# A fused two-block transformer kernel: one 512-column matmul for two of 256 in the up and down stages

## The chip, the cores and the metric

The kernel runs on one core of one Trainium2 chip. The metric is the device time of one execution in microseconds (us). The kernel before took 1595.41 us, the median of three runs. A core has a matrix engine (PE, with PEld for its weight loads), VectorE (DVE), ScalarE (ACT), GpSimd (POOL) and a queue (SP) that issues the weight transfers. TensorE's clock has two levels here, 1.2 and 2.4 GHz; the profile gives it as the granted share, 0.50 or 1.00.

## What is computed

256 tokens of width 1024 go through four layers of attention and gated feed-forward, and then through a second block of one layer. The part that the change touches is the feed-forward:

```python
def conv_gated_ffn(h, w_up, conv_w, conv_b, w_down):
    u = h @ w_up
    C = u.shape[-1]
    u = lax.conv_general_dilated(u, conv_w[:, None, :].astype(u.dtype), window_strides=(1,),
                                 padding=[(CONV_W - 1, 0)], dimension_numbers=('NWC', 'WIO', 'NWC'),
                                 feature_group_count=C) + conv_b
    gate, val = jnp.split(u, 2, axis=-1)
    return (jax.nn.silu(gate) * val) @ w_down
```

D_FF is 2752 (21.5 tiles of 128) in these four layers. In the second block (`conv_ffn`) D_FF is 2816, only the gate passes the three-tap convolution, the activation is a GELU, and the value half multiplies it unconvolved.

## The kernel before

Activations lie transposed: 128 features on the partitions, 256 tokens (S) in a row. All matrix products are made in float32r with both operands split into a high and a low part, `w_hi`, `w_lo` and `h_hi`, `h_lo` (in the down stage `act_hi`, `act_lo`), and three matmuls of 256 columns stand for one product: high by high, high weights by low activations, low weights by high activations. This is `product` (lines 1480, 1481 and 1482); such a group of three is called a triple below, with 128 by 128 weights of its own for each of its matmuls. The first two chunks of an up stage go through `pair` and `first_outputs` (lines 1515 and 1524), which take the tiles of h as they come.

Weights come from memory in 225 chunks, through a ring of three slots (`w_raw`, `w_hi`, `w_lo`). SP loads a chunk when the low part of the chunk three before it is made; ACT copies it to `w_hi` (line 321) when PE has used the chunk three before; DVE subtracts to get `w_lo` (line 804), and PE's `chunk_ready` waits for that. Stages follow one another: mixer projections and attention, `wo` (output projection), `up` (22 chunks), `down` (8 chunks). A chunk of `up` is 16 triples: 8 for a gate tile into a bank of `pj`, 8 for a value tile into a bank of `val_bank`. In the first four layers chunk 21, the last, holds half tiles and is 8 triples. A chunk of `down` is 22 triples into one bank.

Beside PE each chunk of `up` has a step on each engine, with no scheduler: the order is as the code is written, with semaphores. `used` counts finished chunks. ACT's step j writes tap 2 and the bias of both tiles from PSUM to `cgate` and `cval` (line 733), makes the high part of chunk j+3 (`next_split`), and applies Silu to the gate (line 737). DVE's step adds the other two taps of both tiles from PSUM (line 1242, four instructions), makes the low part of chunk j+3, and multiplies gate and value (line 1259). POOL's step (`split_act`, lines 1451 and 1454) makes `act_hi` and `act_lo` of the product. Chunk 0 of `up` was computed from h without its norm factor, so its step first multiplies by `rstd` (line 1234). Steps 1 to 18 lie in a hardware loop of six turns of three steps, on ACT and on DVE; steps 0 and 19 to 21 stand outside it.

PE starts `down` with the first 19 triples of two chunks, and then waits for `act_free`, that is for POOL's last step, before their last three. DVE adds each finished chunk from PSUM to `x` (line 1279); ACT's squares and the next stage's raw h follow it.

## Time and profile before

| | |
|---|---|
| three runs, us | 1595.56, 1595.41, 1593.86 |
| span of the profiled execution | 1593.4 us |
| PE busy | 1536.5 us, 96% |
| DVE busy | 1037.6 us, 65% |
| ACT busy | 861.8 us, 54% |
| POOL busy | 315.3 us, 20% |
| chain that ended last | PE 83%, DVE 9%, ACT 4% |
| DMA | mean 166 GB/s |

The span is the profiled execution's own time; it lies 2.0 us below the median of the runs. Matmuls are pipelined, and the duration of one (283 ns) includes the way through the array, so their rate is read from the distance between starts. The same holds to a lesser degree for DVE and ACT, where neighbours overlap by some 0.08 us.

### The profile page before, as it was taken

The page shows a single profiled execution, that of the slowest core. Times are in us where ns is not written, and L with a number is a line of the kernel's source. Part 1 is how long each engine was busy: PE and PEld are TensorE (multiplying, and loading weights), DVE is VectorE, ACT ScalarE, POOL GpSimd, SP SyncE. Part 2 cuts the span into 40 slices and gives each one's busy share as a digit, 9 for nine tenths or more (in the row PEclk, how much of TensorE's full clock was granted, in tenths as well). Part 3 has the DMA queues.
Part 4 walks back from the last instruction along what each step waited for, and adds up shares of the span by engine and source line. Part 5 has one row for each costly group of instructions (what it writes and reads, how often), then busy time and mean ns, then how long its engine had stood idle before and what let it go on. Part 6 is the DMA issues. An engine that isn't in the chain of part 4 may idle for free.

```text
span 1593.4 us, 32385 instructions
## 1 busy us (share of the span) xinstructions
PE 1536.5 (96%) x12270; PEld 1483.0 (93%) x12270; DVE 1037.6 (65%) x1639; ACT 861.8 (54%) x1347; POOL 315.3 (20%) x474
## 2 busy tenths in 40 slices
PE   6999999999999999989999999999999897899998
PEld 5989999999999999978999999899999897899997
DVE  5668876553378765567877466688765655866555
ACT  4766555455565554455656446665554455544533
POOL 2103211212222112112212220022110360211100
PEclk9999999999999999999999999999999899899999
DMA  7543556443336564442656445435564253355550
GB/s 256 169 159 117 205 183 241 152 159 118 119 113 207 183 243 152 132 159 80 211 184 219 178 148 167 160 116 205 182 243 152 96 196 106 129 188 194 189 205 27
DMA packets 36669, 264.70 MB, mean 166 GB/s; under 512 B 4767, under 2 KB 4826, under 8 KB 7792
## 3 DMA queue, kind: packets, MB, share of 16 engines
q1 hardware_dynamic: 33552, 255.59, 45.8%
q0 software_dynamic: 3040, 8.05, 2.0%
q8 instruction: 52, 0.85, 0.2%
q14 instruction: 25, 0.20, 0.0%
HBM read 262.50 MB, written 1.12 MB: 165 GB/s over the span
## 4 chain that ended last, share of the span: by engine, by line
PE 83%; DVE 9%; ACT 4%; issue 2%; DMA 1%; SPq 0%; POOL 0%; ACTq 0%; DVEq 0%
PE bank L1480 26%; PE bank L1481 24%; PE bank L1482 24%; PE bank L1515 2%; DVE w_lo L804 2%; DVE tmp L853 2%; ACT tmp L395 1%; PE bank L1524 1%; DVE acc L841 1%; PE bank L1623 1%; ACT w_hi L321 1%; DVE tmp L885 1%; PE bank L1591 1%; DVE w_lo L813 1%; DMA w_raw<-w_std 1%
## 5 line engine op out<-in xcount | busy, mean ns | idle before, releaser
L804 DVE TENSOR_TENSOR w_lo<-w_raw,w_hi 128x2048 fp32r<-128x2048 f32 (+2 forms) x220 | 543.3, 2472 | 221.4 <-ACT w_hi L321 221.2
L1480 PE MATMUL bank<-h_hi,w_hi 128*128 128x256 f32 x2032 | 579.0, 285 | 1.3 <-DVE w_lo L804 1.3
L1481 PE MATMUL bank<-h_lo,w_hi 128*128 128x256 f32 x2032 | 574.9, 283 | 0.0
L1482 PE MATMUL bank<-h_hi,w_lo 128*128 128x256 f32 x2032 | 574.9, 283 | 0.0
L321 ACT CAST w_hi<-w_raw 128x2048 fp32r<-128x2048 f32 (+2 forms) x220 | 445.2, 2024 | 5.7 <-DMA w_raw<-w_std 2.9
L1480 PEld LDWEIGHTS bank<-h_hi,w_hi 128*128 128x128 f32 x2032 | 389.6, 192 | 6.7 <-issue 4.1
L1481 PEld LDWEIGHTS bank<-h_lo,w_hi 128*128 128x128 f32 x2032 | 389.7, 192 | 0.1
L1482 PEld LDWEIGHTS bank<-h_hi,w_lo 128*128 128x128 f32 x2032 | 389.6, 192 | 0.0
L1480 PE MATMUL bank<-act_hi,w_hi 128*128 128x256 f32 x1220 | 355.9, 292 | 5.7 <-DVE act_lo L957 4.2
L1481 PE MATMUL bank<-act_lo,w_hi 128*128 128x256 f32 x1220 | 345.7, 283 | 0.0
L1482 PE MATMUL bank<-act_hi,w_lo 128*128 128x256 f32 x1220 | 345.5, 283 | 0.0
L1480 PEld LDWEIGHTS bank<-act_hi,w_hi 128*128 128x128 f32 x1220 | 233.9, 192 | 20.1 <-DVE act_lo L957 6.0
L1481 PEld LDWEIGHTS bank<-act_lo,w_hi 128*128 128x128 f32 x1220 | 234.4, 192 | 0.1
L1482 PEld LDWEIGHTS bank<-act_hi,w_lo 128*128 128x128 f32 x1220 | 234.5, 192 | 0.0
L733 ACT ACTIVATE tmp<-bank,par 128x256 f32<-128x256 f32 x181 | 93.6, 562 | 227.9 <-PE bank L1482 227.3
L1242 DVE SCALAR_TENSOR_TENSOR tmp<-bank,par,tmp 128x255 f32<-128x255 f32 (+1 forms) x362 | 155.6, 478 | 85.0 <-ACT tmp L733 82.3
L1451 POOL CAST act_hi<-tmp 128x256 f32 x110 | 43.6, 397 | 482.6 <-DVE tmp L1259 372.3
L351 ACT ACTIVATE sq<-x 128x256 f32<-128x256 f32 (+1 forms) x67 | 31.9, 479 | 166.7 <-DVE x L1279 154.7
L1353 POOL TENSOR_SCALAR proj<-x,par 128x256 f32<-128x256 f32 x35 | 44.4, 1270 | 327.7 <-ACT h_hi L379 327.7
L1515 PE MATMUL bank<-h_hi,w_hi 128*128 128x256 f32 x320 | 94.0, 312 | 12.8 <-ACT h_hi L375 7.3
L1515 PE MATMUL bank<-h_hi,w_lo 128*128 128x256 f32 x320 | 90.3, 301 | 0.0
L1454 POOL TENSOR_TENSOR act_lo<-tmp,act_hi 128x256 f32 x110 | 81.4, 740 | 17.6 <-POOL act_hi L1451 17.2
(162 smaller groups left out, 1754.1 us busy)
## 6 DMA issues: line engine op xcount, KB each, us to landing
w_raw<-w_std SPq DMA_DIRECT2D x181, 1024.0 KB, 4.9
w_raw<-w_down SPq DMA_DIRECT2D x40, 1408.0 KB, 6.0
w_raw<-w_gate SPq DMA_DIRECT2D x4, 1280.0 KB, 5.4
act_hi<-vec_dram POOLq DMA_DIRECT2D x28, 128.0 KB, 3.1
act_lo<-vec_dram POOLq DMA_DIRECT2D x28, 128.0 KB, 3.6
x<-xT SPq DMA_DIRECT2D x2, 512.0 KB, 4.7
out<-x SPq DMA_DIRECT2D x4, 256.0 KB, 2.4
par<-params SPq DMA_DIRECT2D x1, 499.0 KB, 9.3
```

The costliest lines, as they stand in the source:

```text
L321: act.copy(w_hi[:, slot, 0:width], w_raw[:, slot, 0:width]).then_inc(hi_ready, 1)
L351: act.activation(sq[:, n, to:end], source, ACT.Square).then_inc(sq_ready, 1)
L733: act.activation(to[:, slot, :], source, ACT.Identity, bias=col(3), scale=col(2)).then_inc(conv_init, 1)
L804: dve.tensor_tensor(w_lo[:, slot, 0:width], w_raw[:, slot, 0:width], w_hi[:, slot, 0:width].bitcast(F32), ALU.subtract).then_inc(lo_ready, 1)
L1242: return dve.scalar_tensor_tensor(to[:, slot, lag:S], source(v)[:, 0:S - lag], par[:, bass.ds(at + (4 * v + 2 - lag), 1)], to[:, slot, lag:S],
L1353: pool.tensor_scalar(proj[:, k % 4, :], x[:, k, :], gain_of(app, k), None, ALU.mult)\
L1451: pool.tensor_copy(act_hi[:, bass.ds(j, 1), :].squeeze(1) if not isinstance(j, int) else act_hi[rows, j, :], cval[rows, slot, :]).then_inc ...
L1454: pool.tensor_tensor(act_lo[rows, j, :], cval[rows, slot, :], act_hi[rows, j, :].bitcast(F32), ALU.subtract).then_inc(act_free, 1)
L1480: pe.matmul(dst, wh, xh, start=first, stop=False, skip_group_check=shared)
L1481: pe.matmul(dst, wh, xl, start=False, stop=False, skip_group_check=shared)
L1482: done = pe.matmul(dst, wl, xh, start=False, stop=last, skip_group_check=shared)
L1515: pe.matmul(dst, a, b, start=k == 0 and w is wh and (n == 0 or not shared), stop=False, skip_group_check=shared)
```

## The change

- `h_hi` and `h_lo`, and `act_hi` and `act_lo`, become halves of one tensor each (`h_both`, `act_both`), so that high and low lie side by side as 512 columns. `wide_product` makes a triple from two matmuls: low weights by the high 256 columns, then high weights by all 512. The second leaves high by high in the left half of a bank and high by low in the right half. It is used in all `up` stages and in the `down` stages of the first four layers: 4 x 344 + 352 = 1728 triples of `up` and 4 x 176 = 704 of `down`, 2432 in all.
- `pj` and `val_bank` are interleaved, so that a chunk's two banks are neighbours. In `up`, ACT first copies both right halves to `up_sum` (512 columns, signal `low_taken`), DVE adds both left halves (512 columns, signal `bank_free`), and bias, taps and the value read SBUF. In `down`, DVE adds the two halves to `x` one after the other.
- DVE no longer multiplies gate and value; POOL does, ahead of its two split instructions.
- DVE's step makes the low part of the chunk two ahead, not three, and makes it ahead of the taps. Step 0 makes none, and one more stands behind step 21.
- ACT's Silu of tile j-1 is now in step j, between the copy and the bias instructions.

The new helper on PE:

```diff
+            def wide_product(bank, weights, moving, start, stop):
...
+                for k, ((wh, wl), (xh, pair)) in enumerate(zip(weights, moving)):
+                    pe.matmul(bank[:, 0:S], wl, xh, start=start and k == 0, stop=False, skip_group_check=True)
+                    done = pe.matmul(bank[:, :], wh, pair, start=False, stop=stop and k == len(weights) - 1,
+                                     skip_group_check=True)
+                return done
```

ACT's step in `up`:

```diff
+                            act.copy(up_sum[:, slot, :, :], halves(slot, S)).then_inc(low_taken, 1)
+                        if before is not None:
+                            activate(*before)
+                        if isinstance(j, int) and j == 0:
+                            act.wait_ge(first_scaled, ffn + 1)
+                        else:
+                            act.wait_ge(bank_free, c + (RING + 1))
...
+                            act.activation((cgate, cval)[v][:, slot, :], up_sum[:, slot, v, :], ACT.Identity,
...
                         split()
```

DVE's step in `up`:

```diff
+                        dve.wait_ge(low_taken, n_ + 1)
...
+                            dve.tensor_tensor(up_sum[:, slot, :, :], halves(slot, 0), up_sum[:, slot, :, :], ALU.add)\
+                               .then_inc(bank_free, 1)
                         if first:
...
+                            dve.tensor_tensor(up_sum[:, slot, :, :], up_sum[:, slot, :, :],
+                                              rstd[:, :].unsqueeze(1).broadcast_to([P, 2, S]), ALU.mult)\
+                               .then_inc(first_scaled, 1)
+                        split()
...
+                    def split_two_ahead(j, i=None):
+                        n_ = c0 + j + 2
+                        split_lo(n_ if i is None else i * RING + n_, n_ % RING, SIZES[n_])
```

DVE in `down`, and POOL's step in `up`:

```diff
                             dve.tensor_tensor(x[:, k, :], pj[slot_of(c0, k)][:, 0:S], x[:, k, :], ALU.add)\
+                               .then_inc(x_main, 1)
+                            dve.wait_ge(x_main, layer * DT + k + 1)
+                            dve.tensor_tensor(x[:, k, :], pj[slot_of(c0, k)][:, S:2 * S], x[:, k, :], ALU.add)\
                                .then_inc(bank_free, 1)
...
+                        pool.wait_ge(gated, n_ + 1)
...
+                        pool.tensor_tensor(cval[rows, slot, :], cgate[rows, slot, :], value, ALU.mult)\
+                            .then_inc(prod_done, 1)
```

One step of DVE in the loop of `up`, before (`bank` is PSUM, `tmp` holds `cgate` and `cval`):

```order
L1242 SCALAR_TENSOR_TENSOR tmp<-bank,par,tmp 128x255
L1248 REGISTER_ALU
L1242 ISA [waits conv_init]
L1242 SCALAR_TENSOR_TENSOR tmp<-bank,par,tmp 128x255
L1250 ISA
L1242 ISA [waits conv_part]
L1242 SCALAR_TENSOR_TENSOR tmp<-bank,par,tmp 128x254
L1253 REGISTER_ALU
L1242 ISA [waits conv_part]
L1242 SCALAR_TENSOR_TENSOR tmp<-bank,par,tmp 128x254
L803 REGISTER_ALU
L804 TENSOR_TENSOR w_lo<-w_raw,w_hi 128x2048 [waits hi_ready]
```

The same step of DVE with the change (`held` holds `up_sum`):

```order
L1237 TENSOR_TENSOR held<-psum,held 128x512 [waits low_taken]
L817 REGISTER_ALU
L818 TENSOR_TENSOR w_lo<-w_raw,w_hi 128x2048 [waits hi_ready]
L1260 ISA
L1248 ISA [waits conv_init]
L1248 SCALAR_TENSOR_TENSOR tmp<-held,par,tmp 128x255
L1260 REGISTER_ALU
L1248 ISA [waits conv_init]
L1248 SCALAR_TENSOR_TENSOR tmp<-held,par,tmp 128x255
L1263 ISA
L1248 ISA [waits conv_part]
L1248 SCALAR_TENSOR_TENSOR tmp<-held,par,tmp 128x254
```

The sum and the weights' low part stand ahead of the taps, the taps read SBUF alone, and the multiplication (L1259, the row behind the first piece) is gone.

ACT at the end of step 0 and in the first step of the loop of `up`, before:

```order
L733 ACTIVATE tmp<-u_sb,par 128x256 [waits first_scaled]
L321 CAST w_hi<-w_raw 128x2048 [waits arrived1,used]
L737 ACT_TABLE_LOAD
L737 ACTIVATE tmp<-tmp 128x256 [waits conv_part]
L744 UNCONDITIONAL_BRANCH
L744 ISA
L724 REGISTER_ALU [waits used]
L733 ISA [waits act_free]
L733 ISA
L733 ACTIVATE tmp<-bank,par 128x256
```

The same place with the change:

```order
L747 ACTIVATE tmp<-held,par 128x256
L331 CAST w_hi<-w_raw 128x2048 [waits arrived1,used]
L757 UNCONDITIONAL_BRANCH
L757 ISA
L734 REGISTER_ALU [waits used]
L738 ACT_TABLE_LOAD
L738 COPY held<-psum 128x512 [waits act_free]
L726 ISA
L727 ACT_TABLE_LOAD
L727 ACTIVATE tmp<-tmp 128x256 [waits conv_part]
```

The one table load that stood ahead of the loop has become two inside it, which every turn runs again.

The end of `up` on DVE, before; the three rows of `w_lo` with 2816 columns are the first three chunks of `down`:

```order
L1242 SCALAR_TENSOR_TENSOR tmp<-bank,par,tmp 128x255 [waits conv_init] x2
L1242 SCALAR_TENSOR_TENSOR tmp<-bank,par,tmp 128x254 [waits conv_part] x2
L804 TENSOR_TENSOR w_lo<-w_raw,w_hi 128x2816 [waits hi_ready]
L1259 TENSOR_TENSOR tmp<-tmp 128x256 [waits bank_free,gated]
L1242 SCALAR_TENSOR_TENSOR tmp<-bank,par,tmp 128x255 [waits conv_init] x2
L1242 SCALAR_TENSOR_TENSOR tmp<-bank,par,tmp 128x254 [waits conv_part] x2
L804 TENSOR_TENSOR w_lo<-w_raw,w_hi 128x2816 [waits hi_ready]
```

The same with the change:

```order
L1237 TENSOR_TENSOR held<-psum,held 128x512 [waits low_taken]
L818 TENSOR_TENSOR w_lo<-w_raw,w_hi 128x2048 [waits hi_ready]
L1248 SCALAR_TENSOR_TENSOR tmp<-held,par,tmp 128x255 [waits conv_init] x2
L1248 SCALAR_TENSOR_TENSOR tmp<-held,par,tmp 128x254 [waits conv_part] x2
L1237 TENSOR_TENSOR held<-psum,held 128x512 [waits low_taken]
L818 TENSOR_TENSOR w_lo<-w_raw,w_hi 128x2816 [waits hi_ready]
L1248 SCALAR_TENSOR_TENSOR tmp<-held,par,tmp 128x255 [waits conv_init] x2
L1248 SCALAR_TENSOR_TENSOR tmp<-held,par,tmp 128x254 [waits conv_part] x2
L1234 TENSOR_TENSOR held<-psum,held 128x256 [waits low_taken]
```

The first pieces of both begin with step 19. The first chunk of `down` was split in step 19 and is now split in step 20.

## Rows read from the trace of the kernel before

**Rows 1.** The page: span, and busy time of each engine.

```profile
span 1593.4 us, 32385 instructions
PE 1536.5 (96%) x12270; PEld 1483.0 (93%) x12270; DVE 1037.6 (65%) x1639; ACT 861.8 (54%) x1347; POOL 315.3 (20%) x474
```

**Rows 2.** Groups by line and shape: count, then busy us, mean ns, idle before.

```profile
L443 ACT COPY vtok<-bank 128x512 f32<-128x512 f32 x15 | 8.5, 570 | 4.0 <-PE bank L1482 4.0
...
L1175 DVE TENSOR_TENSOR x<-bank,x 128x512 f32<-128x512 f32 x12 | 7.9, 685 | 7.6 <-PE bank L1482 7.6
...
L737 ACT ACT_TABLE_LOAD x5 | 6.4, 1283 | 0.1
```

**Rows 3.** Timeline of PE in an up stage: start, duration; 48 matmuls between starts.

```profile
250.08 0.28 PE L1480 MATMUL bank<-h_hi,w_hi 128*128 128x256 f32 x1
...
255.84 0.28 PE L1480 MATMUL bank<-h_hi,w_hi 128*128 128x256 f32 x1
```

**Rows 4.** Timeline of PEld: weight loads of plain float32 matmuls, and the next load.

```profile
1258.45 0.84 PEld L1591 LDWEIGHTS bank<-sq,cst 128*128 128x128 f32 x4
1259.31 0.19 PEld L1515 LDWEIGHTS bank<-h_hi,w_hi 128*128 128x128 f32 x1
```

**Rows 5.** Timeline of PE: two float32r matmuls while the granted clock is 0.50.

```profile
745.58 0.41 PE L1515 MATMUL bank<-h_hi,w_lo 128*128 128x256 f32 x1
745.80 0.41 PE L1515 MATMUL bank<-h_hi,w_hi 128*128 128x256 f32 x1
```

**Rows 6.** Timeline of DVE: one whole step of the loop of up.

```profile
161.29 1.65 DVE L1242 SCALAR_TENSOR_TENSOR tmp<-bank,par,tmp 128x255 f32<-128x255 f32 x4
162.85 2.28 DVE L804 TENSOR_TENSOR w_lo<-w_raw,w_hi 128x2048 fp32r<-128x2048 f32 x1
165.05 0.42 DVE L1259 TENSOR_TENSOR tmp<-tmp 128x256 f32<-128x256 f32 x1
```

**Rows 7.** Timeline of POOL as up begins in layer 0.

```profile
148.02 0.75 POOL L1341 TENSOR_TENSOR h_lo<-tmp,h_hi 128x256 fp32r<-128x256 f32 x1 [0.80 <-ACT h_hi L375]
```

**Rows 8.** Timeline of DVE as up begins in layer 0 (brackets: idle before).

```profile
148.10 2.82 DVE L804 TENSOR_TENSOR w_lo<-w_raw,w_hi 128x2048 fp32r<-128x2048 f32 x1
150.85 0.74 DVE L1234 TENSOR_TENSOR u_sb<-bank,rstd 128x256 f32<-128x256 f32 x2
...
154.31 2.29 DVE L804 TENSOR_TENSOR w_lo<-w_raw,w_hi 128x2048 fp32r<-128x2048 f32 x1 [0.53 <-ACT w_hi L321]
```

**Rows 9.** Timeline of ACT as up begins in layer 0, and in step 20.

```profile
151.38 1.10 ACT L733 ACTIVATE tmp<-u_sb,par 128x256 f32<-128x256 f32 x2 [3.43 <-DVE u_sb L1234]
152.38 1.90 ACT L321 CAST w_hi<-w_raw 128x2048 fp32r<-128x2048 f32 x1
...
260.72 1.02 ACT L733 ACTIVATE tmp<-bank,par 128x256 f32<-128x256 f32 x2 [1.99 <-PE bank L1482]
```

**Rows 10.** Timeline of DVE, step 19: the first chunk of down.

```profile
258.45 3.09 DVE L804 TENSOR_TENSOR w_lo<-w_raw,w_hi 128x2816 fp32r<-128x2816 f32 x1 [1.18 <-ACT w_hi L321]
```

**Rows 11.** Timeline of POOL: the end of its step in the loop of up.

```profile
161.54 0.40 POOL L1451 CAST act_hi<-tmp 128x256 f32 x1 [3.11 <-DVE tmp L1259]
162.10 0.74 POOL L1454 TENSOR_TENSOR act_lo<-tmp,act_hi 128x256 f32 x1 [0.16 <-POOL act_hi L1451]
```

**Rows 12.** Stretches: length, busy us of each engine (count), PEclk, DMA share, GB/s.

```profile
157.00:265.00 108.00, 108.00 (x902) 108.00 (x902) 84.79 (x119) 63.37 (x80) 22.77 (x40) 1.00 0.58 202
...
741.30:744.30 3.00, 1.35 (x5) 0.59 (x4) 2.42 (x5) 1.65 (x5) 2.43 (x3) 1.00 0.38 161
744.40:747.50 3.10, 3.10 (x12) 2.92 (x13) 2.88 (x4) 2.18 (x4) 0.00 (x0) 0.50 0.00 0
747.70:751.00 3.30, 3.30 (x29) 3.30 (x28) 3.30 (x7) 2.26 (x6) 1.83 (x2) 0.98 0.71 228
```

**Rows 13.** Timeline of DVE in down, layer 0: two additions to x in a row.

```profile
285.30 0.42 DVE L1279 TENSOR_TENSOR x<-bank,x 128x256 f32<-128x256 f32 x1
...
292.05 0.42 DVE L1279 TENSOR_TENSOR x<-bank,x 128x256 f32<-128x256 f32 x1
```

212 lines of the change are left out of this document (103 added, 109 removed).

## Prediction

> **What bounds the kernel now.** I read the page first: PE is busy 96% of the span of 1593.4 us [rows 1]. Then the stretches: in 108 us of the up stage of layer 0 PE has no idle time at all, while DVE is busy 85 us, ACT 63 and POOL 23 [rows 12]. So in `up` a saved PE nanosecond is gained until DVE's own work for a chunk is longer than PE's. The timelines give both. PE: 48 matmuls, one chunk, lie between 250.08 and 255.84, so 5.76 us a chunk, 0.120 a matmul, 0.360 a triple [rows 3]. DVE: the taps take 1.56 us from start to start, the low part of the weights 2.20 [rows 6]. The sums below are of one profiled execution; its span is 2.0 us below the median of the runs, and I add that back at the end.
>
> **A triple on PE.** The columns stay 768, and a weight load goes. At the granted clock of 0.50 two matmuls start 0.22 us apart, close to 256 columns at 1.2 GHz (0.213) [rows 5]. At 2.4 GHz 256 columns would be 0.107, but the row has 0.120: here something other than columns adds 13 ns [rows 3]. Whether it adds them to 512 columns too, no float32r row tells. The nearest are the four plain float32 matmuls, which start 0.86/4 = 0.215 us apart at full clock, with a weight load each: as long as 512 columns take (0.213), with only 2 ns above them [rows 4]. So I take 0.216 for the wide one and 0.120 for the narrow: 0.336 a triple, 24 ns less. The ends are 0.213 (0.333) and, if the extra is in proportion to the columns, 0.240 (0.360, no gain); between them lies 0.227 (0.347), a fixed 13 ns. Over 2432 triples the 24 ns would be 58 us.
>
> The Trainium skill (TensorE: Matmul & The Clock Gate, Back-to-back issue gap) gives N/2.4 + 2.5 ns for matmuls in a row. By it 256 columns take 109 ns and 512 take 216, and this change would bring only 2.5 ns a triple, 6 us in all. For 256 columns the trace disagrees (120), so its rule against the change falls for the narrow ones; for 512 no run here shows it yet.
>
> **DVE's step in up.** It loses the multiplication and gains a sum of 512 columns: 0.685 us by its group, 0.60 without the overlap of neighbours [rows 2]. So 0.60 + 2.20 + 1.56 = 4.36 us, against PE's 16 x 0.336 = 5.38. But the taps now read SBUF twice, not PSUM, and POOL has a third instruction. A POOL subtraction starts at 148.02 and takes 0.75; DVE's instruction with two SBUF inputs starts at 148.10 and takes 2.82, not 2.28 [rows 7, 8]. So POOL held it up for 0.54 us, until 0.62 after its own start. In `up` before, POOL's two lie beside taps from PSUM, which keep their pace (1.65 for four) [rows 6, 11]. Now two such POOL instructions and a cast (0.40, perhaps 0.3 of it) can delay DVE by up to 1.5 a step; the least is 0. The product mostly begins while DVE is in the sum, which reads PSUM, so I take 1.0: 5.36, a tie with PE. With the table loads below I take **5.45 us a chunk** for chunks 2 to 20; the ends are 5.38 and 5.8.
>
> **ACT.** The order of instructions shows two table loads in the loop where one stood ahead of it: 1.283 us each [rows 2], 2.6 us in three steps. ACT had 63 busy of 108 us, and its step grows by a 512-column copy (0.57 [rows 2]) and 0.85 of loads: from 3.4 to 4.8 of 5.4 us. It hides, except where ACT's copy releases DVE: one sum in three comes 1.3 us later.
>
> **The start of up.** After the low part of chunk 2 is ready at 150.85, PE works on it for 5.76, until 156.6; that of chunk 3 is ready at 154.31 + 2.2 = 156.5, just in time [rows 8]. Now it stands in step 1, behind this chain from 150.85: DVE sum and scaling of 512 columns 1.3; ACT's two bias instructions 1.0 and high part 1.9 [rows 9]; table load 1.3; copy 0.55; DVE's sum 0.65; low part 2.2. That is 8.9, against 5.4 for PE's chunk: **a wait of 3.5 us** in each of layers 0 to 3, and 3.0 in layer 4, which has one bias instruction. Chunks 0 and 1 gain nothing: the low part of chunk 2 is late behind them already.
>
> **The end of up.** Chunk 20 ends at 260.7 [rows 9], and the first chunk of `down` is ready at 258.45 + 3.0 = 261.5, 2.1 us before PE has done the half chunk 21 [rows 10]. Now its low part is made in step 20: copy 0.6, sum 0.65, 3.0, so 4.3 after chunk 20, where PE is done after 2.7. The wait is 1.6 if DVE is in time, and 3.1 to 3.7 if it lags. I take **2.5**, in layers 0 to 3 only: layer 4 has a whole chunk 21. POOL's longer last step is hidden by PE's 2 x 19 triples, 12.8 us.
>
> **Down.** 176 x 0.024 = 4.2 us less in each of four layers. DVE's and ACT's round there is 292.05 - 285.30 = 6.75, and 7.1 with the second addition [rows 13]; PE's chunk of 22 triples falls to 7.4 and covers it. Behind the last chunk PE has the next stage's raw tiles, except after layer 3: there the addition adds 0.4.
>
> **The clock.** After 3 us in which PE was busy 1.35, the granted clock was 0.50 for 3.1 us: 12 matmuls instead of 26 [rows 12]. One such fall costs 1.6 us. A wait of 3.5 should bring it in all five layers; in four of them DVE catches up meanwhile, so I count 1.2 there. For the wait at the end I count half of it, 0.8.
>
> **The sum.** A layer of the first four: 19 x (5.45 - 5.76) = -5.9; chunk 21 -0.2; down -4.2; start +3.5; end +2.5; clock +2.0: together -2.3, times four -9.2. Layer 4: 20 x 0.384 = -7.7, start +3.0, clock +1.6: -3.1. End of layer 3 +0.4. Together -11.9: a span of 1581.5, and 1583.5 beside the median. The case's own range is 1574 to 1592.
>
> **Rivals.**
> - **POOL makes DVE the bound (slower).** The delay is 1.4 a step: 5.75 us a chunk. Then 19 chunks give -0.2, the end wait is 3.7, and the clock at the start costs nothing more: -0.2 - 0.2 - 4.2 + 3.5 + 3.7 + 0.8 = +3.4 a layer, +13.6, and with layer 4 and the 0.4 about +11: 1606. It decides from 5.6 us a chunk on, since each 0.1 is 7.6 us. For it: the 0.54 us of delay [rows 7, 8]. Against: only if all three POOL instructions meet DVE's. Chance 0.18. The Trainium skill (SBUF — State Buffer, Who interferes with whom) has the rule: a DVE instruction with two SBUF inputs and a GpSimd instruction that reads SBUF exclude each other for the whole instruction; the trace agrees, with 0.62 of 0.75 us.
> - **The wide matmul costs 0.240.** Nothing is gained on PE; the waits stay (3.1, 1.5, clock 1.9 a layer; 4.2 in layer 4): +31, 1626. Against it: the 0.215 us [rows 4]. Chance 0.07.
> - **It costs 0.227.** Chunks at 5.55: -4.0 - 0.1 - 2.3 + 3.3 + 2.1 + 1.7 = +0.7 a layer, layer 4 about 0, and 0.4: +3, 1599, at the edge of no change. Chance 0.14.
> - **No contention and no clock fall to speak of.** 5.38 a chunk, end wait 1.6: -7.3 - 0.2 - 4.2 + 3.5 + 1.6 = -6.6 a layer, -26; layer 4 -4.7: -31, 1565; with the falls at the start 1573. Chance 0.24.
>
> The forecast has 0.37. Faster by over 0.2% (under 1592.2; about what a measurement can tell from no change): 0.55, the forecast but for its edge and the last rival. Within 0.2%: 0.13. Slower: 0.32, from the first two and half of the third. The range is 1565 to 1609; it leaves out the second rival and the ends of the first and last.
>
> **What would show it.** Wide matmuls followed by the next start after 0.216 us; used chunks 5.4 to 5.5 apart in `up`; PE waiting some 3.5 us for `w_lo` ahead of chunk 3 in five layers, and 2 to 3 us ahead of `down` in four; a granted clock of 0.50 behind them; 60 table loads of 1.28 us in the loops; low parts of 2.8 us on DVE where POOL is at work. The prediction is wrong if DVE never idles in `up`, or if the wide matmuls start 0.24 apart.

## The result, and the profile after

The changed kernel took **1609.5 us**, the median of four runs (1608.2 to 1610.5), beside 1595.3 for the kernel before (four runs, 1593.9 to 1595.6). The ratio is 1.0091, with a 95% interval of 1.0077 to 1.0105: slower by 0.9%, 14 us. The prediction had 1583.5 and "faster". The page after, its span and busy times, against [rows 1]:

```profile
span 1608.7 us, 27907 instructions
PE 1523.7 (95%) x9838; PEld 1348.0 (84%) x9838; DVE 1166.1 (72%) x1666; ACT 1006.1 (63%) x1512; POOL 584.1 (36%) x584
```

PE has 2432 matmuls fewer and is busy for 13 us less in a span that is 15 us longer. So PE waits more, and what it does takes longer than was forecast.

**PE's price.** Its timeline in `up` of layer 1, in two stretches of the same stage (start, duration; of each triple its narrow matmul, the first of its two):

```profile
500.04 0.28 PE L1501 MATMUL psum<-h_both,w_lo 128*128 128x256 f32 x1
...
500.73 0.28 PE L1501 MATMUL psum<-h_both,w_lo 128*128 128x256 f32 x1
...
560.13 0.28 PE L1501 MATMUL psum<-h_both,w_lo 128*128 128x256 f32 x1
...
561.19 0.28 PE L1501 MATMUL psum<-h_both,w_lo 128*128 128x256 f32 x1
```

Around 500 two triples take 0.69 us, and over a chunk 5.55: 0.347 a triple. From the start of a narrow matmul to that of the wide one are 0.117 us, from there to the next narrow one 0.230. Around 560 three triples take 1.06 us: 0.353, or 5.66 a chunk; there the wide matmul has 0.236. Before, a triple took 0.360 [rows 3]. The prediction took 0.336. The two distances, 5.55 and 5.66 us a chunk, are called the short and the long cadence below.

**The waits.** PE's waits for the low parts of the weights, over the whole span (us in all, times, longest of them). The four that the view puts down to "issue" are those ahead of `down`:

```profile
PE psum L1501 <- DVE w_lo L818: 16.3, 8, 3.3
...
PE psum L1501 <- issue: 9.4, 4, 2.4
```

Windows of PE in layer 0: ahead of chunk 3 and behind it; then in layer 1: ahead of `down` and behind its start (busy us and count of PE, PEld, DVE, ACT, POOL; then the granted clock):

```profile
156.00:159.50 3.50, 0.76 (x5) 0.40 (x3) 2.42 (x2) 3.46 (x6) 0.55 (x1) 1.00 0.00 0
159.50:163.00 3.50, 2.97 (x10) 2.59 (x11) 3.50 (x6) 2.95 (x4) 2.23 (x4) 0.51 0.54 152
588.90:591.60 2.70, 0.36 (x3) 0.06 (x2) 2.70 (x2) 2.70 (x2) 2.70 (x1) 1.00 0.55 234
593.00:596.40 3.40, 3.40 (x13) 2.81 (x12) 3.40 (x4) 2.63 (x3) 2.41 (x1) 0.50 0.88 358
```

The first wait is 3.2 to 3.3 us in layers 0 to 3 and 2.6 in layer 4, the second 2.4 in layers 0 to 3. Behind the first of layers 0, 1 and 2 and behind all four of the second there are 3.4 us at a granted clock of 0.50 (1.2 GHz), in which PE does half its work: 1.4 to 1.8 us more each. None of these nine waits is in the kernel before.

The chain of the first wait, on DVE and ACT in layer 0 (brackets: idle before, and its releaser):

```profile
150.81 0.68 DVE L1237 TENSOR_TENSOR held<-psum,held 128x512 f32<-128x512 f32 x1
...
157.08 0.69 DVE L1237 TENSOR_TENSOR held<-psum,held 128x512 f32<-128x512 f32 x1 [2.42 <-ACT held L738]
157.69 2.28 DVE L818 TENSOR_TENSOR w_lo<-w_raw,w_hi 128x2048 fp32r<-128x2048 f32 x1
```

```profile
155.17 1.28 ACT L738 ACT_TABLE_LOAD   x1
156.46 0.59 ACT L738 COPY held<-psum 128x512 f32<-128x512 f32 x1
```

It is the chain of the prediction: 157.69 + 2.2 = 159.9 is 9.1 us behind 150.81 (8.9 forecast), while PE has work for 5.55.

**DVE in `up`**, one step of the steady state, and POOL beside it:

```profile
538.30 2.60 DVE L818 TENSOR_TENSOR w_lo<-w_raw,w_hi 128x2048 fp32r<-128x2048 f32 x1
540.82 2.34 DVE L1248 SCALAR_TENSOR_TENSOR tmp<-held,par,tmp 128x255 f32<-128x255 f32 x4
543.08 0.68 DVE L1237 TENSOR_TENSOR held<-psum,held 128x512 f32<-128x512 f32 x1
543.68 2.60 DVE L818 TENSOR_TENSOR w_lo<-w_raw,w_hi 128x2048 fp32r<-128x2048 f32 x1
```

```profile
543.39 0.74 POOL L1459 TENSOR_TENSOR tmp<-tmp 128x256 f32<-128x256 f32 x1 [1.30 <-ACT tmp L727]
544.30 2.24 POOL L1462 CAST act_both<-tmp 128x256 f32 x1 [0.17 <-POOL tmp L1459]
546.72 0.74 POOL L1465 TENSOR_TENSOR act_both<-tmp,act_both 128x256 f32 x1 [0.18 <-POOL act_both L1462]
```

From one low part to the next are 5.38 us: the low part takes 2.60 and the four taps 2.34, where they took 2.28 and 1.65 [rows 6]. POOL's product (543.39) delays the low part by 0.3, its subtraction (546.72) the taps by 0.7. The cast delays nobody, but is itself held up while DVE makes the low part: 2.24 us instead of 0.40 [rows 11]. The Trainium skill (SBUF — State Buffer, Who interferes with whom) says that a DVE instruction with two SBUF inputs contends with a GpSimd instruction that reads SBUF, and that the lock is exclusive. The trace agrees for POOL's product and subtraction, in both directions; the cast is shut out (2.24 us), but shuts nobody out.

That step has no table load. A turn of the loop, three steps, has two. DVE's sums behind the load, in two turns in a row of layer 1, and PE at the chunk whose low part ends at 538.30 + 2.60 = 540.90:

```profile
515.44 0.69 DVE L1237 TENSOR_TENSOR held<-psum,held 128x512 f32<-128x512 f32 x1 [0.30 <-ACT held L738]
...
532.13 0.69 DVE L1237 TENSOR_TENSOR held<-psum,held 128x512 f32<-128x512 f32 x1 [0.30 <-ACT held L738]
```

```profile
541.03 0.31 PE L1501 MATMUL psum<-h_both,w_lo 128*128 128x256 f32 x1
...
541.40 0.28 PE L1501 MATMUL psum<-h_both,w_lo 128*128 128x256 f32 x1
```

A turn takes 16.69 us, 5.56 a chunk, where 5.45 was forecast, and in it (504 to 541) neither ACT nor DVE waits for PE. Three short chunks of PE are 16.64. So while PE keeps the short cadence, DVE with ACT's table loads is as much the bound of `up` as PE: the first triple of chunks 7, 10 and 13 takes 0.37 to 0.40 us for 0.347. In the long cadence (16.97) DVE has 0.3 us in hand.

**Stage by stage.** PE's first matmul of `up`, of `down`, and of the next stage, in layer 1, before and after:

```profile
458.78 0.78 PE L1515 MATMUL bank<-h_hi,w_hi 128*128 128x256 f32 x1
...
582.41 0.28 PE L1480 MATMUL bank<-act_hi,w_hi 128*128 128x256 f32 x1
...
648.66 0.38 PE L1515 MATMUL bank<-h_hi,w_hi 128*128 128x256 f32 x1
```

```profile
463.25 0.74 PE L1543 MATMUL psum<-h_both,w_lo 128*128 128x256 f32 x1
...
591.61 0.36 PE L1501 MATMUL psum<-act_both,w_lo 128*128 128x256 f32 x1 [2.35 <-issue]
...
657.74 0.38 PE L1546 MATMUL psum<-h_both,w_hi 128*128 128x256 f32 x1
```

`up` went from 123.6 to 128.4 us, `down` from 66.3 to 66.1. Layer 0 has +5.1 and -0.3. In all, layers 0 to 3 bring 4.8, 4.3, 4.3 and 4.0 us, and the rest of the program -2.1 (before, layer 4 begins with 17.1 us at the lower clock; after, with 10.2 and 3.4): 15.3 us of span.

### The profile page after: what moved, and what is told of

It is laid out like the page before. It is cut to its first block, busy times and chain, and to the rows that moved or that the text cites. A ratio compares the mean times of both kernels' runs of the same rounds, so it can differ in the third digit from the quotient of the medians.

```text
span 1608.7 us, 27907 instructions
## 1 busy us (share of the span) xinstructions
PE 1523.7 (95%) x9838; PEld 1348.0 (84%) x9838; DVE 1166.1 (72%) x1666; ACT 1006.1 (63%) x1512; POOL 584.1 (36%) x584
## 4 chain that ended last, share of the span: by engine, by line
PE 75%; DVE 14%; ACT 6%; issue 4%; DMA 1%; POOL 0%; ACTq 0%; SPq 0%; DVEq 0%
PE psum L1502 32%; PE psum L1501 17%; PE psum L1491 7%; PE psum L1492 7%; PE psum L1493 7%; DVE w_lo L818 4%; DVE tmp L867 3%; ACT w_hi L331 1%; ACT tmp L405 1%; DVE acc L855 1%; PE psum L1655 1%; DVE tmp L899 1%; DVE h_both L863 1%; DVE w_lo L827 1%; DMA w_raw<-w_std 1%
## 5 line engine op out<-in xcount | busy, mean ns | idle before, releaser
L1502 PE MATMUL psum<-h_both,w_hi 128*128 128x512 f32 x1568 | 556.0, 399 | 0.0
L1501 PE MATMUL psum<-h_both,w_lo 128*128 128x256 f32 x1568 | 443.1, 283 | 16.3 <-DVE w_lo L818 16.3
L1502 PEld LDWEIGHTS psum<-h_both,w_hi 128*128 128x128 f32 x1568 | 296.5, 189 | 71.7
L1501 PEld LDWEIGHTS psum<-h_both,w_lo 128*128 128x128 f32 x1568 | 298.2, 190 | 20.3 <-DVE w_lo L818 19.8
L1502 PE MATMUL psum<-act_both,w_hi 128*128 128x512 f32 (+1 forms) x704 | 254.0, 400 | 0.0
L1248 DVE SCALAR_TENSOR_TENSOR tmp<-held,par,tmp 128x255 f32<-128x255 f32 (+1 forms) x388 | 242.2, 673 | 6.6 <-ACT tmp L747 3.4
L1501 PE MATMUL psum<-act_both,w_lo 128*128 128x256 f32 (+1 forms) x704 | 206.5, 293 | 9.4 <-issue 9.4
L1462 POOL CAST act_both<-tmp 128x256 f32 x110 | 178.2, 1620 | 18.9 <-POOL tmp L1459 18.5
L1491 PE MATMUL psum<-act_both,w_hi 128*128 128x256 f32 x516 | 150.4, 292 | 5.8 <-DVE act_both L971 4.1
L1492 PE MATMUL psum<-act_both,w_hi 128*128 128x256 f32 x516 | 146.4, 284 | 0.0
L1491 PE MATMUL psum<-h_both,w_hi 128*128 128x256 f32 x464 | 135.1, 291 | 0.9 <-DVE w_lo L818 0.9
L1492 PE MATMUL psum<-h_both,w_hi 128*128 128x256 f32 x464 | 131.2, 283 | 0.0
L1493 PE MATMUL psum<-h_both,w_lo 128*128 128x256 f32 x464 | 131.1, 283 | 0.0
```

Of the source, the lines that this page charges most:

```text
L1248: return dve.scalar_tensor_tensor(to[:, slot, lag:S], up_sum[:, slot, v, 0:S - lag], par[:, bass.ds(at + (4 * v + 2 - lag), 1)], to[:, slo ...
L1462: pool.tensor_copy(act_hi[:, bass.ds(j, 1), :].squeeze(1) if not isinstance(j, int) else act_hi[rows, j, :], cval[rows, slot, :]).then_inc ...
L1491: pe.matmul(dst, wh, xh, start=first, stop=False, skip_group_check=shared)
L1492: pe.matmul(dst, wh, xl, start=False, stop=False, skip_group_check=shared)
L1493: done = pe.matmul(dst, wl, xh, start=False, stop=last, skip_group_check=shared)
L1501: pe.matmul(bank[:, 0:S], wl, xh, start=start and k == 0, stop=False, skip_group_check=True)
```

## The experiments

The theory, **edges**: PE is still the bound inside `up`; the wide matmul saves 7 to 13 ns a triple and not 24; and the loss is made at the two edges of each `up`, where the later low parts make PE wait and its clock falls. The rivals: **DVE**, slowed by POOL, has become the bound of `up`; or **ACT**, by its table loads, has. The times are medians of four executions (ten for e1 and e5, seven for e3 and e9, five for e8), and each ratio is to runs of the kernel before on the same chip. Waits, clock falls and cadences are those of the one profiled execution. The diffs are cut to what matters; comments in them are added.

| run | edit | us | ratio to before (95%) |
|---|---|---|---|
| changed kernel | | 1609.5 | 1.0091 (1.0077, 1.0105) |
| e1 | start of `up`: chunk 3 split in step 0 | 1593.2 | 0.9990 (0.9979, 1.0001) |
| e2 | end of `up`: low parts earlier | 1614.3 | 1.0135 (1.0109, 1.0161) |
| e3 | e1 and e2 | 1601.0 | 1.0045 (1.0027, 1.0063) |
| e4 | wide matmuls as two of 256 (not in chunks 0 and 1 of `up`) | 1625.6 | 1.0200 (1.0181, 1.0218) |
| e5 | no table loads in the loop | 1593.9 | 0.9996 (0.9985, 1.0006) |
| e6 | DVE multiplies | 1606.6 | 1.0064 (1.0039, 1.0089) |
| e7 | wide matmuls in `down` alone | 1588.0 | 0.9953 (0.9937, 0.9970) |
| e8 | e1 and e6 | 1589.5 | 0.9960 (0.9946, 0.9974) |
| e9 | e1 and e5 | 1590.0 | 0.9967 (0.9955, 0.9978) |
| e10 | e9, end of `up` on ACT and DVE | 1579.6 | 0.9904 (0.9887, 0.9920) |
| e11 | POOL's product twice | 1634.1 | 1.0243 (1.0226, 1.0260) |
| e12 | e10, one wait more | 1579.2 | 0.9893 (0.9868, 0.9917) |
| e13 | e12 again | 1576.3 | 0.9887 (0.9870, 0.9903) |
| e14 | e12, matmuls in the other order | 1583.1 | 0.9926 (0.9910, 0.9943) |

### e1: the start

```diff
 ACT, step 0
                         act.copy(up_sum ...)
+                        split()                       # high part of chunk 3
                         act.wait_ge(first_scaled, ffn + 1)
...
-                        split()
 DVE
-                    step(0, ..., lambda: None)
+                    step(0, ..., lambda: split_two_ahead(1))
+                    step(1, ..., lambda: None)
-                        for k in range(1, RING + 1):
+                        for k in range(2, RING + 2):
```

> The changed kernel (1609.5 us, span 1608.7) with one edit at the start of up: in step 0 ACT makes the high part of chunk 3 ahead of the bias instructions, DVE makes its low part behind the scaling, and step 1 makes none; all later steps are as they were. Theory, edges: PE is the bound inside up, and what the change lost are two waits a layer with a clock fall behind each. The start costs 3.2 us of waiting and 1.6 of half clock in layers 0 to 3, and about as much in layer 4: 5 x 4.8 = 24 us fewer at most, 20 if layer 4 keeps its fall: 1586 to 1590, the wait ahead of down stays at 2.4 us. Rival, DVE: DVE with its busy 98 of 102 us is the bound of up; the low part that is now earlier puts its step behind, PE waits 0.5 to 2 us inside up or more at the end: the gain is under half, 1598 or more. Rival, nothing: the chain is as long as before because DVE waits for ACT anyway: 1609.

1593.2 us, 16 less: short of the 20 to 24 expected, and more than either rival allows. The waits ahead of chunk 3 and the three clock falls behind them are gone. What is left (the same view as above):

```profile
PE psum L1505 <- issue: 9.3, 4, 2.4
...
PE psum L1505 <- DVE w_lo L821: 6.3, 8, 1.4
```

In each of the first four layers a wait of 1.2 to 1.4 us has come up ahead of chunk 4. The low part in step 0 makes DVE late for step 1, so the DVE rival holds for one chunk, not for the stage: the later chunks take 5.66. The sum, from the starts of chunks 2 to 5: 3.2 to 3.3 us in each of layers 0 to 2 (the wait shorter by 1.9, the rest the clock fall), 2.1 in layer 3, where no fall was to be saved, and 2.5 in layer 4. One fall ahead of `down` is gone too (1.6), and twelve chunks that had been short are long (less 1.3). That is 15, as the profiled spans have it (15.3).

### e2 and e3: the end, first try

```diff
                     for j in range(turns * RING + 1, n):
-                        step(j, ..., lambda: split_two_ahead(j))
-                    split_two_ahead(n)
+                        step(j, ..., lambda: split_two_ahead(j) if j < n - 2 else None)
+                        if j >= n - 3:
+                            split_two_ahead(j + 1)
```

> The changed kernel (1609.5 us) with one edit at the end of up: the low parts of the first three chunks of down are made behind the taps of steps 19, 20 and 21, as in the kernel before, and not ahead of the taps of steps 20 and 21 and behind step 21. Theory, edges: the wait of 2.4 us and the half clock behind it (1.6) go in four layers: 16 us fewer, 1593 to 1595. The wait at the start stays at 3.2. Rival, DVE: with the taps ahead of the low part the bias instruction (0.8 us of waiting) stands in the way and DVE is late with the second chunk of down or PE waits for the last products: half of the gain or less, 1601 or more.

1614.3 us: dearer by 0.44%, where a gain of 1% was expected. The wait ahead of `down` fell only from 2.4 to 1.4 us. The reason is in POOL and ACT in layer 1:

```profile
588.61 3.36 POOL L1460 TENSOR_TENSOR tmp<-tmp 128x256 f32<-128x256 f32 x1 [1.30 <-ACT tmp L727]
```

```profile
592.02 1.09 ACT L747 ACTIVATE tmp<-held,par 128x256 f32<-128x256 f32 x2 [3.58 <-DVE held L1237]
593.02 2.53 ACT L331 CAST w_hi<-w_raw 128x2816 fp32r<-128x2816 f32 x1
```

The low part, now ahead of the sum of step 20, holds back that sum by 3.0 us; ACT's bias waits 3.6 for it, and the high part of the second chunk stands behind the bias. POOL's product takes 3.4 us instead of 0.7, shut out by the low part. So two waits have taken the place of the one (low parts 17.8 us in 12 waits, up from 16.3 in 8; POOL):

```profile
PE psum L1502 <- POOL act_both L1466: 6.1, 4, 1.6
```

The edges failed. What the second theory said is what happened: the bias stands in the way, and PE waits for the last products; its 1601 or more holds too, by far. The clock shows what the edges had right. None of the eight waits (1.4 to 1.6 us) has a fall behind it, and `down` still takes 66.9 us for 66.1, since the waits inside it cost more than the fall. Layer 4, which the edit leaves as it was at its start, had a fall here (1.5 us) that it hadn't before. The end is no matter of one instruction's place.

> The changed kernel with both edits, at the start of up and at its end. Theory, edges: no wait for w_lo and no clock fall behind one is left in the first four layers; the two gains add: 24 + 16 = 40 us fewer, 1570 to 1574, which is below the kernel before (1595.3) by about 22: 2432 triples at 7 to 13 ns are 16 to 32. Rival, DVE: DVE has no slack left in up, so the low parts that are made earlier come back as waits inside up: 1585 or more, and PE's chunks in up are longer than 5.66 us in the mean.

1601.0 us, and not 1570 to 1574. The gain of the start is there and so is the loss of the end (0.55% above e1), so the edits add, but the second with its own sign. From chunk 5 on no chunk of `up` took more than 5.68 us (5.64 in the mean), so the rival that the earlier low parts come back as waits inside `up` fails.

### e4: the wide matmul's price

```diff
-                    done = pe.matmul(bank[:, :], wh, pair, ...)
+                    pe.matmul(bank[:, 0:S], wh, pair[:, 0:S], ...)
+                    done = pe.matmul(bank[:, S:2 * S], wh, pair[:, S:2 * S], ...)
```

> The changed kernel with every 512-column matmul of wide_product written as two of 256 with the same weights, into the same two halves of the bank; all else as it was. Theory, edges: a triple goes back to 0.360 us from 0.347 (0.353 in much of up), 2432 triples cost 16 to 32 us more, of which the waits give back some 3 because PE needs its weights later: 1622 to 1638. Rival, DVE: DVE's step is the bound of up, PE's longer chunks are hidden there and only the 704 triples of down show: 1614 to 1618. Rival, the wide matmul brings nothing: 1609.

1625.6 us, 16 more; triples take 0.360, in every stage. The sum: the edit reaches 2272 triples (chunks 0 and 1 go through another helper), and by 13 ns they are 30 us; 71 chunks of the changed kernel had the long cadence and lose only 0.1 (less 7.5); the waits are 0.2 to 0.3 shorter, since PE asks for its weights later (less 2), and three clock falls fewer lie behind those ahead of `down` (less 5): 15 to 16. So the wide matmul is worth some 22 us in these triples, and the theory's forecast holds. Two matmuls of 256 columns in a row with the same weights still take 0.120 each; each has a weight load of its own in the trace, so what a load kept for both would save isn't shown. Three narrow matmuls cost 40 ns above their columns at 2.4 GHz (0.360 for 0.320), a narrow and a wide one 27 (0.347). That is 13 ns a matmul at either width in the sum, neither the 2 ns that the prediction read from plain float32 [rows 4] nor an extra in proportion to the columns, which would leave 0.360. How the 27 are shared the starts don't say: they have 0.117 and 0.230, that is 10 and 17.

### e5: the table loads

```diff
+                    step(1, c0 + 1, ..., lambda: next_split(c0, 1), (0, slot_of(c0, 0)))
-                    turns = (n - 1 - RING) // RING
+                    turns = (n - 1 - RING) // RING - 1
-                        for k in range(1, RING + 1):
+                        for k in range(2, RING + 2):
```

> The changed kernel (1609.5 us) with ACT's step 1 taken out of the loop of up, whose turns become five (steps 2 to 16); the engine's state is then the same on entry and on each turn, and no table load stands in the loop: one of 1.28 us is left ahead of it, behind the copy of step 1. Theory, edges: inside up PE is the bound and the 60 loads cost nothing; only the copy of step 1 comes 1.3 us earlier, so the wait ahead of chunk 3 falls from 3.2 to 1.9 in five layers: 6.5 us fewer, 1603, a little less if some clock falls go too (1598). Rival, ACT: the loads (2.6 us in every three steps) hold back the sum, and with it DVE and PE; without them 15 us or more go: below 1594. Rival, nothing: 1609.

1593.9 us, 16 less, at least 4 more than the edges expected (6.5 to 11.5), and where the ACT rival had its mark. ACT and DVE behind chunk 2 of layer 0, then a window of layer 1 around the wait:

```profile
155.23 0.56 ACT L738 COPY held<-psum 128x512 f32<-128x512 f32 x1
155.81 1.28 ACT L727 ACT_TABLE_LOAD   x1
```

```profile
155.83 0.69 DVE L1238 TENSOR_TENSOR held<-psum,held 128x512 f32<-128x512 f32 x1 [1.00 <-ACT held L738]
```

```profile
474.00:477.50 3.50, 1.65 (x10) 1.20 (x9) 3.50 (x4) 3.49 (x5) 1.94 (x2) 1.00 0.01 2
```

The chain is shorter by the load ahead of the copy, as expected: the wait is 1.8 to 1.9 us, not 3.3, and in layer 4 1.3, not 2.6. What was not expected lies in the clock and the cadence. The clock stays at 1.00 behind the shorter wait, as in the window, in three of the four layers (in layer 2 it fell), and behind the waits ahead of `down` (2.1 us) it fell in two of four: three falls for seven. And four of the five `up` stages ran at 5.55 us a chunk, 51 chunks more than in the changed kernel. The sum: at the starts of the five stages 9 us, ahead of `down` 1 and behind it 3, by the short chunks 5 to 6; the profiled spans differ by 18.7 (1590.0; it is the second fastest execution of the ten, which spread over 8 us).

So the ACT rival is right in part. In the short cadence the loads held PE up themselves, but only by 0.03 to 0.05 us every third chunk (layer 1 of the changed kernel, above). The larger part goes by way of the cadence. In the changed kernel each change from the short cadence to the long one (chunk 13 of layer 1, chunk 7 of layers 2 and 3) stands at such a held-up triple, of 0.360 to 0.383 us. Over all runs, 4 of 31 stages with loads in the loop ran short from chunk 5 to their end (those of layers 0 to 3 of e11 left out), and 16 of 30 without. The runs without loads differ in other edits, too, so that the loads bring on the long cadence is likely and not shown.

### e6 and e8: POOL's product back on DVE

```diff
+                    def multiply(j, slot): ...       # on DVE, behind the low part of step j + 1
-                        pool.tensor_tensor(cval[rows, slot, :], cgate[rows, slot, :], value, ALU.mult)
```

> The changed kernel (1609.5 us) with the product of gate and value made by DVE again: the product of tile j-1 stands in DVE's step j behind the low part, and one more behind step 21; POOL makes only act_hi and act_lo. All else as it was. Theory, edges with POOL's lock as a cause of DVE's lateness: DVE's step gains 0.34 us and loses the 0.55 us or more by which the product holds up a low part or two taps; PE's pace in up stays at 5.55 to 5.66 us a chunk, the wait at the start stays 3.2, the wait at the end falls from 2.4 to about 2: 1604 to 1609. Rival, POOL is the bound of up: chunks of 5.65 become 5.55 and the end wait goes: 1594 or less. Rival, DVE's added instruction makes it the bound: 1615 or more.

1606.6 us. DVE's sum in two steps in a row:

```profile
174.28 0.69 DVE L1246 TENSOR_TENSOR held<-psum,held 128x512 f32<-128x512 f32 x1 [0.29 <-ACT held L738]
...
179.66 0.68 DVE L1246 TENSOR_TENSOR held<-psum,held 128x512 f32<-128x512 f32 x1
```

The step is 5.38 us, as without the edit: the product costs DVE 0.34 as its own work and 0.3 as a lock. The waits at the start stay at 3.2 to 3.3, and three of the four ahead of `down` fall to 1.9, as expected. The 3 us less than the changed kernel lie within the spread of the four executions (1602.6 to 1609.6).

> The edit of e1_start (1593.2 us: high and low part of chunk 3 in step 0) together with DVE's multiplication of e6. In e1 PE still waits 1.4 us ahead of chunk 4 and 2.3 us ahead of down in each of the first four layers, with a low part of 2.6 us and four taps of 2.33 in each step of DVE, against 2.28 and 1.65 in the kernel before. Theory, POOL's lock: POOL's product stands against DVE's work on SBUF in each step; without it DVE's step is shorter by 0.2 to 0.5 us and both waits shrink: 2 to 8 us fewer, 1585 to 1591. Rival, the order alone sets the waits (copy, sum, low part of 3 us behind used chunk 20): no change, 1593. Rival, DVE's extra instruction: 1597 or more.

1589.5 us. The waits for low parts fall from 6.3 us to 3.5, those ahead of `down` from 9.3 to 8.0. This is the lower half of what the lock was expected to bring, near the line of no change; by the medians the product's place is worth 3 to 4 us.

### e7: `down` alone

The kernel before, with the wide matmuls in `down` of layers 0 to 3:

```diff
                             dve.tensor_tensor(x[:, k, :], pj[slot_of(c0, k)][:, 0:S], x[:, k, :], ALU.add)\
+                               .then_inc(x_main, 1)
+                            dve.wait_ge(x_main, layer * DT + k + 1)
+                            dve.tensor_tensor(x[:, k, :], pj[slot_of(c0, k)][:, S:2 * S], x[:, k, :], ALU.add)\
                                .then_inc(bank_free, 1)
...
+                            done = wide_product(pj[slot], weights, hidden, a == 0, b == FT)
```

> The kernel before (1595.3 us) with the wide matmuls in the down stages of the first four layers alone: act_hi and act_lo are halves of one tensor, DVE adds both halves to x; up is as it was before, with its order, its multiplication on DVE and its low parts three ahead. Theory, edges: 704 triples at 13 ns are 9.2 us, no wait is added since up is untouched, and the second addition (0.45) shows only behind layer 3: 1586 to 1588. Rival: the second addition makes DVE late with the next low part and PE waits in down: 1593 or more. Rival, the wide matmul saves 24 ns when DVE and POOL are idle: 1579.

1588.0 us, 7 less than before, as expected, and no wait of `up` or ahead of `down` has come up. PE's first matmuls of `down` and of the next stage in layer 1:

```profile
580.30 0.28 PE L1492 MATMUL bank<-act_both,w_lo 128*128 128x256 f32 x1
...
644.84 0.38 PE L1527 MATMUL bank<-h_hi,w_hi 128*128 128x256 f32 x1
```

64.54 us for 66.25: 1.7 a layer, where 176 x 13 ns are 2.3; the first 30 to 40 triples have the long cadence here. So this part of the change is a gain by itself. DVE's second addition (0.45) shows behind layer 3 alone, as the theory had it: there 1.25 us of the 1.7 are left.

### e9, e10 and e12: both edges

> The edit of e1 (high and low part of chunk 3 in step 0) and that of e5 (no table load in the loop) together; each alone gave 1593 to 1594. Theory, edges and loads: e5 has left a wait of 2.1 us at the start (no clock fall), and 2.0 to 2.4 at the end; with chunk 3 ready early there is at most the wait ahead of chunk 4 (1.2 us in e1, less without the load in step 1): 1 to 2 us a layer fewer than e5, and the end stays: 1584 to 1589. Rival: the two edits remove the same wait, and the low part in step 0 makes DVE late at chunk 4 by as much: 1592 to 1594. Rival, full sum: 1578 (16.3 + 15.6 us below 1609.5).

1590.0 us, just above the 1584 to 1589 expected: e1 and e5 remove the same wait, so their gains don't add. Left are 1.1 us ahead of chunk 4 and 2.1 ahead of `down`.

e10 moves the high parts too, so that nothing that ACT owes DVE stands behind a wait for DVE:

```diff
 ACT, steps 20 and 21
                         act.copy(up_sum ...)
+                        if late:
+                            split()
                         activate(*before)
 DVE
+                    step(n - 3, ..., lambda: split_two_ahead(n - 3), lambda: split_two_ahead(n - 2))
+                    step(n - 2, ..., lambda: split_two_ahead(n - 1))
+                    step(n - 1, ..., lambda: None)
                     split_two_ahead(n)
```

> e9 with a third edit, at the end of up: the low part of the first chunk of down stands between the taps of step 19, that of the second ahead of the taps of step 20, that of the third behind step 21; ACT makes the high parts in steps 20 and 21 ahead of Silu and bias. e2, which moved the low parts without moving the high ones, cost 5 us, since ACT's high part waited behind bias for DVE, and POOL's product was held up for 3.4 us by each low part. Theory, edges: the wait of 2 us ahead of down goes in four layers and with it some clock falls (1.6 each): 8 to 12 us below e9, 1574 to 1580. Rival, POOL at the end: the last products come late because each low part of 3 us holds POOL up, and PE waits for act_lo behind 2 x 19 triples instead: no gain on e9, 1584 to 1590.

1579.6 us, 10 below e9, as the edges had it (the profiled execution, 1584.0, is the slowest of four, and its span only 4 below that of e9). The wait ahead of `down` is gone and with it its clock falls. One of 1.1 us for POOL is left, the rival's mechanism in small. e12 lets DVE wait for POOL's last step (`act_free`) ahead of the last low part:

> e10 (1579.6 us) with one wait more: in the first four layers DVE begins the low part of the third chunk of down only when POOL has finished its last step. In e10 this low part (588.61, 3.08 us) holds POOL's last product up (589.63, 2.65 us instead of 0.7), and PE waits 1.1 us for act_lo. Theory, POOL's lock at the end: the last product takes 0.7, act_lo is ready 1.4 to 2 us earlier, before PE asks for it, and the low part is ready at about 594.4 where PE needs it at 595: 4 x 1.1 = 4 to 5 us fewer, 1575. Rival: the low part comes too late and PE waits for it by as much: 1579 to 1582.

POOL's last product in layer 1, in e10 and then in e12, with DVE's low part of e12:

```profile
589.63 2.65 POOL L1472 TENSOR_TENSOR tmp<-tmp 64x256 f32<-64x256 f32 x1 [1.22 <-ACT tmp L723]
```

```profile
589.71 0.73 POOL L1474 TENSOR_TENSOR tmp<-tmp 64x256 f32<-64x256 f32 x1 [1.22 <-ACT tmp L723]
```

```profile
591.74 3.09 DVE L825 TENSOR_TENSOR w_lo<-w_raw,w_hi 128x2816 fp32r<-128x2816 f32 x1 [2.98 <-POOL act_both L1480]
```

The wait is gone in all four layers: `down` takes 64.4 us for 65.7, and no fall of the clock is left in or ahead of it. Yet the median is 1579.2, no different from e10 within the interval, and the 1575 expected wasn't reached. In the profiled execution four stages had the long cadence, in e10's two; each costs up to 2 us.

### e11: how far POOL is from making DVE the bound

```diff
+                        pool.tensor_tensor(extra[rows, slot, :], cgate[rows, slot, :], value, ALU.mult)
                         pool.tensor_tensor(cval[rows, slot, :], cgate[rows, slot, :], value, ALU.mult)
```

> The changed kernel (1609.5 us) with POOL's product made twice in each step of up (first into a tile of its own that nobody reads): one more POOL instruction of 0.74 us on two SBUF operands beside DVE. It sizes the rival of the prediction by which POOL makes DVE the bound. Theory: DVE's step is 5.37 us where nothing makes it wait, against 5.55 to 5.66 of PE, so DVE is no bound in the changed kernel but only 0.2 to 0.3 short of one; one more lock of 0.3 to 0.6 us takes it to 5.7 to 5.95: 95 chunks at 0.1 to 0.3 more, and a later end: 1622 to 1642. Rival, the product is hidden behind the sum, which reads PSUM: 1609 to 1612. Rival, DVE is the bound already: each 0.5 us of lock shows in full, 1655.

1634.1 us. DVE's step, and PE's waits for low parts (30, where the changed kernel has 8):

```profile
522.32 0.68 DVE L1238 TENSOR_TENSOR held<-psum,held 128x512 f32<-128x512 f32 x1
...
525.12 3.33 DVE L1249 SCALAR_TENSOR_TENSOR tmp<-held,par,tmp 128x255 f32<-128x255 f32 x4
...
528.37 0.68 DVE L1238 TENSOR_TENSOR held<-psum,held 128x512 f32<-128x512 f32 x1
```

```profile
PE psum L1503 <- DVE w_lo L819: 22.0, 30, 3.3
```

Chunks take 5.88 in the mean in layers 0 to 3, as expected. The rival of the prediction is real as a mechanism. In a step without a table load DVE has 0.2 us in hand before it; over a whole turn with its loads it has none against the short cadence (16.69 for 16.64 us) and 0.3 against the long one.

### e13 and e14: the two cadences

> The kernel of e12 once more, unchanged, to see whether a stage's cadence belongs to the program or to the execution. In e12's profile the chunks of up took 5.66 us in layers 0, 1, 2 and 4 and 5.55 in layer 3; in e10's it was 5.66 in layers 0 and 3 only. If the cadence is chosen anew in each execution: another set of layers has 5.66, and the times spread again by some 5 us (1574 to 1582). If it belongs to the program: the same four layers.

1576.3 us. The same program had 5.66 in layer 1 alone, and not in layers 0, 1, 2 and 4. So the cadence of an `up` stage is chosen in the execution, not by the program. PE at the same place in e12 and in e13, three triples each:

```profile
199.94 0.28 PE L1516 MATMUL psum<-h_both,w_lo 128*128 128x256 f32 x1
...
201.00 0.28 PE L1516 MATMUL psum<-h_both,w_lo 128*128 128x256 f32 x1
```

```profile
199.95 0.28 PE L1516 MATMUL psum<-h_both,w_lo 128*128 128x256 f32 x1
...
200.99 0.28 PE L1516 MATMUL psum<-h_both,w_lo 128*128 128x256 f32 x1
```

> The kernel of e12 with the two matmuls of a wide triple in the other order: high weights by both halves first, then low weights by the high half. The columns, the weight loads and all waits are as they were. If the longer cadence (0.353 us a triple for 0.347) is a matter of how the two matmuls follow one another on PE: one cadence only, 0.347 everywhere, 1573 to 1575, or a new one for all stages. If it is contention with the other engines for SBUF or comes from them: the same mixture of 5.55 and 5.66, 1574 to 1582.

1583.1 us, dearer by 0.3 to 0.4%. The mixture is still there (four stages at 5.66, layer 3 at 5.55), so the order of the two matmuls isn't its cause. Part of `down` has the long cadence, too, in either order, but more of it in this one (`down` takes 64.5 to 64.8 us for 64.4). Most stages keep one cadence from chunk 5 on. A few went from the short one to the long one on the way, each at a chunk whose first triple was held up (0.36 to 0.38 us), and none back. So PE seems to take its cadence anew where it is held up; which of the two it takes stays open. Between e12 and e13, the same program, the five `up` stages differ by 5.5 us in all, of 7.7 us between the two spans. It isn't seen with three matmuls of 256 columns: there every chunk takes 5.76.

## Why the prediction was wrong

By its own terms, a layer of the first four, as predicted and as measured (layer 0, with e12 for `down` without its clock fall; a wait at the start is chunk 2's 9.08 us less 5.66):

| term | predicted | measured |
|---|---|---|
| chunks 2 to 20, without waits | -5.9 | -1.9 |
| chunk 21 | -0.2 | -0.1 |
| `down` | -4.2 | -1.9 |
| wait at the start | +3.5 | +3.4 |
| wait at the end | +2.5 | +2.4 |
| half clock, start and end | +1.2, +0.8 | +1.4, +1.6 |
| sum | -2.3 | +4.9 |

Layers 0 to 3 came out at +17.4 together, against -9.2 (layer 3 had no clock fall at the start, layers 1 to 3 some short chunks), and all else at -2.1, against -2.7: 27 us of span, the miss.

- **The step that failed is the price of a triple**: "So I take 0.216 for the wide one". It was read from plain float32 matmuls [rows 4], and PE's own row of them shows that they were no 512-column matmuls:

```profile
1258.66 1.03 PE L1591 MATMUL bank<-sq,cst 128*128 128x256 f32 x4
```

They are 256 columns wide, and each of the four takes 0.215 us, twice what its columns need. They take as long as 512 columns would, and tell nothing of a 512-column matmul in float32r. The narrow row of the same data type [rows 3] had 13 ns on each matmul. The pair measured 0.347, so a triple saved 13 ns (7 in the long cadence), not 24. With 0.347 the prediction's own third rival had 1599. The formula of the Trainium skill (TensorE: Matmul & The Clock Gate, Back-to-back issue gap), which the section calls that of an isolated matmul, has 109 ns for 256 columns and 216 for 512; the trace has 120 for a narrow one among its like, and 347 for one of each together, where an estimate by the formula has 325. Its conclusion, that little is gained, was nearer than the 24 ns that were taken.
- **DVE's step with the table loads** was the second term too small: 5.45 taken, 5.56 measured over a turn. So by an estimate from these rows, chunks 2 to 20 would have gained 19 x 0.2 = 3.8 us at most and not 5.9, even with a triple of 0.336.
- **The long cadence** stood in no term: 0.1 us in most chunks of `up`, up to 2 us a layer.
- **Clock**: at the start the discount was right. Layer 3, which had no fall, shows what a fall hides: PE waits for the low part of chunk 4 instead (0.24 us), chunk 3 takes 5.90 for 7.04 to 7.20, and a fall costs 1.1 to 1.3 net, where 1.2 was counted. At the end all four layers had a fall, at 1.6 to 1.8 us each (`down` 65.9 to 66.1 for the 64.4 of e12), where half of one was counted.
- **Table loads**: that they hide is true in the long cadence alone. The one at the start was in the 8.9 us at its right price; that two of the three clock falls at the start hang on it (e5) was missed.
- **Right**: both waits, in place and size (3.5 and 2.5 against 3.4 and 2.4); DVE's step without a load (5.36 against 5.38); POOL's lock (1.0 against 0.3 + 0.7). The rival that POOL makes DVE the bound gave 1606, near the result, by a size that didn't come: it had chunks of 5.75, and DVE's turns brought 5.56.
- **Not tried**: a start of `up` without the wait ahead of chunk 4, and the wide form in `down` of layer 4.

The version that beats both kernels is e12: the changed kernel with edits of order around the same arithmetic, 1576 to 1579 us in two sets of runs (e13 is the same program), 1.1% below the kernel before.

## What to carry to other kernels

A price is read from a row of the same data type, and before a row of another type stands in for a width, its own shape is looked at. A fixed cost at one width is the first guess at another. When a change takes work from the engine that is the bound and moves other work later, its loss sits at the ends of the stages, not in their middle: write down for the first and the last chunk what stands ahead of each operand, on every engine, and where the work of one engine stands behind a wait for another. A gain on the bound of some 1.4% (22 us, e4) was eaten by two waits a stage; putting each early instruction where it no longer waits for its consumer got it back.
